# A sparse expert layer in passes of 32 slots on four column tiles, in place of 64 slots on two

## The chip, the cores and the metric

The kernel runs on one core of one Trainium2 chip, as one launch. The metric is the device time of that core in microseconds (us). All data are float32. The profile names the engines PE (TensorE), DVE (VectorE), ACT (ScalarE), POOL (GpSimd) and SP (SyncE, which here only issues DMAs).

## The reference

The model is two blocks over 256 tokens of width 1024. The first block ends in a mixture of 32 experts, of which each token takes 4; the second block is two attention layers, each with an MLP. Only the mixture matters here:

```python
def moe(h, w_router, b_router, w_gate, b_gate, w_up, b_up, w_down, b_down):   # h: 256 x 1024
    logits = h @ w_router + b_router                       # 256 x 32
    top_logit, top_idx = top_k(logits, 4)
    gates = softmax(top_logit)
    # for every expert e, on the tokens xb that chose it:
        g = min(xb @ w_gate[e] + b_gate[e], 7)             # w_gate[e], w_up[e], w_down[e]: 1024 x 1024
        u = clip(xb @ w_up[e] + b_up[e], -7, 7)
        act = g * sigmoid(1.702 * g) * (u + 1)
        y = act @ w_down[e] + b_down[e]
    # y * gate is added to the token's row
```

The 1024 pairs of token and expert are spread unevenly. Counted with the reference's own routing on its inputs, the experts 0 to 31 are chosen by 22, 29, 25, 37, 37, 5, 12, 32, 47, 41, 54, 24, 25, 51, 35, 13, 28, 55, 32, 30, 68, 10, 39, 41, 23, 39, 36, 36, 33, 21, 11 and 33 tokens. One expert (number 20) has more than 64, and 16 have more than 32. The weights of one expert are 3 matrices of 4 MiB.

## The kernel before

**Passes.** An expert's tokens are worked on in passes of `SLOTS` = 64 slots. The number of passes comes from the data: the routing part (lines 1216 to 1255) counts the tokens of every expert, turns the counts into passes per expert and writes a table from which all engines read their loop bounds. With 64 slots there are 33 passes, two for expert 20.

**One pass on TensorE** (`one_pass`, from line 1422): the first product with w_gate (`expand`, L1402), `gather` of the next pass's tokens by a one-hot matrix (L1370), the product with w_up (L1402), the transpose of the gathered tokens (`turn_x`, L1376), the transpose of this pass's gate matrix (L1438), `combine`, which adds the pass before to its tokens (L1412), the transpose of the activations (L1446), the `biases` that open the next pass's sums (L1383), and the product with w_down (L1456).
**The other engines in a pass.** DVE makes the one-hot matrices (L1518, L1522), clips g (L1529) and u (L1531) and multiplies (L1533, L1536). ACT computes the sigmoid (L1496) and copies out of PSUM: xrow (L1498), xs (L1500), selT (L1503), actT (L1505), y (L1507).

**Weights.** They stream through a ring of ten slots (`ring`), each of 2 MiB, called a part: half of one matrix. An expert is six parts, in the order gate 0 and 1, up 0 and 1, down 0 and 1. The parts 1 to 10 in the order of use (all of expert 0, four of expert 1) are loaded while the routing is computed; the other 182 are issued by SP at L1334. SP takes them strictly in order, and before each it waits until the slot is free: until the *last* pass of the expert two back (parts 0 to 3) or one back (parts 4 and 5) has read the part that lies there. An expert with several passes thus keeps its parts until its last pass reads them. After the last part SP issues the loads for the next stage (L1356 to L1361), once the last pass of expert 30 has ended.

**The end.** The last pass is that of expert 31. Behind it come the copy of y and one more `combine` (L1412 at 1128.87), then the second block.

## Time and profile before

| | |
|---|---|
| median of 3 runs | 1847.85 us (1847.38 to 1848.78) |
| the profiled execution | 1845.13 us |
| its span, first to last instruction | 1843.3 us |
| mean granted TensorE clock | 0.996 |
| PE busy | 1799.4 us, 98% of the span |
| expert stage, first product to the end of the last w_down product | 221.4 to 1128.2 us |
| passes in it | 33 |

Everything outside the span is 1.8 us, and the profiled execution was 2.7 us shorter than the median. A busy PE is not PE at its peak, and the share of busy time does not tell by itself which engine or queue sets the time of a stage; that is read from what each waits for.

### The profile page before, as it was taken

The numbers are of one execution on the slowest core, as the hardware profiler recorded it, in microseconds if no ns is written. First come the engines' busy times: TensorE is split into PE (matmuls) and PEld (weight loads), VectorE is DVE, ScalarE is ACT, GpSimd is POOL, SyncE is SP. The second block draws the span as 40 slices with busy tenths as digits, with TensorE's granted clock in tenths as the row PEclk, the third lists the DMA queues.
The fourth block names the chain that finished last, engine by engine and source line by source line (L and its number), as shares of the span: only waits on it lengthen the run. The fifth ranks groups of instructions, "written<-read, shape, count | busy, mean of one in ns | idle before, by whom it ended". The sixth has DMA issues, their size and how long they took to land. (4 is left out here: it accounts for less than half of the span.)

```text
span 1843.3 us, 23681 instructions
## 1 busy us (share of the span) xinstructions
PE 1799.4 (98%) x9487; PEld 1003.5 (54%) x9488; DVE 605.5 (33%) x1262; ACT 371.8 (20%) x721; POOL 10.9 (1%) x14
## 2 busy tenths in 40 slices
PE   7999899999999999999999999999999999999998
PEld 6757533333333333333333335767995466699843
DVE  1854411111111011011011013544655544345555
ACT  3222411111111111111111113332220033222101
POOL 0000000000000000000000000000000000000001
PEclk9999999999999999999999999999999999999999
DMA  9996699999999999999999999432446443124452
GB/s 379 390 191 271 261 418 430 431 431 431 432 432 431 432 431 431 432 431 432 431 431 431 432 431 329 156 142 92 151 149 241 160 182 137 46 92 149 149 176 98
DMA packets 104495, 558.61 MB, mean 303 GB/s; under 512 B 17128, under 2 KB 33997, under 8 KB 78701
## 3 DMA queue, kind: packets, MB, share of 16 engines
q1 hardware_dynamic: 101876, 553.06, 74.3%
q10 hardware_dynamic: 2554, 4.63, 1.8%
q8 instruction: 47, 0.77, 0.2%
q14 instruction: 18, 0.15, 0.0%
HBM read 552.43 MB, written 5.23 MB: 303 GB/s over the span
## 5 line engine op out<-in xcount | busy, mean ns | idle before, releaser
L1402 PE MATMUL ps<-ring,xs 128*64 128x512 f32 x2112 | 465.5, 592 | 4.9 <-DMA ring<-in_w_up 2.5
L1402 PEld LDWEIGHTS ps<-ring,xs 128*64 128x64 f32 x2112 | 151.3, 137 | 307.6 <-issue 298.2
L1456 PE MATMUL ps<-ring,actT 128*64 128x512 f32 x1056 | 233.9, 595 | 0.0
L2274 PE MATMUL ps<-ring 128*128 128x512 f32 x448 | 192.8, 592 | 0.0
L1529 DVE TENSOR_SCALAR hT<-ps 128x512 f32<-128x512 f32 x33 | 22.8, 692 | 446.0 <-PE ps L1402 446.0
L1456 PEld LDWEIGHTS ps<-ring,actT 128*64 128x64 f32 x1056 | 72.9, 137 | 158.7 <-issue 136.8
L2274 PEld LDWEIGHTS ps<-ring 128*128 128x128 f32 x448 | 84.9, 190 | 105.7 <-issue 105.7
L2010 PE MATMUL ps<-hT,ring 128*128 128x256 f32 x512 | 117.9, 383 | 4.3 <-ACT hT L1654 2.9
L1531 DVE TENSOR_SCALAR hT<-ps 128x512 f32<-128x512 f32 x33 | 22.9, 693 | 263.5 <-PE ps L1402 263.5
L2010 PEld LDWEIGHTS ps<-hT,ring 128*128 128x128 f32 x512 | 94.7, 190 | 23.2 <-issue 5.9
L2228 PE MATMUL ps<-hT,ring 128*128 128x128 f32 x768 | 93.4, 275 | 0.2 <-ACT hT L1654 0.2
L2228 PEld LDWEIGHTS ps<-hT,ring 128*128 128x128 f32 x768 | 89.5, 192 | 0.5 <-ACT hT L1654 0.3
L1507 ACT COPY y<-ps 128x512 f32<-128x512 f32 x33 | 19.3, 586 | 246.5 <-PE ps L1456 246.5
L1412 PE MATMUL ps<-selT,y 64*128 64x256 f32 x544 | 67.9, 389 | 0.7 <-ACT y L1507 0.7
L1500 ACT COPY xs<-ps 128x512 f32<-128x512 f32 x33 | 19.4, 587 | 232.4 <-PE ps L1376 232.4
L1370 PE MATMUL ps<-x_sb,sel 128*64 128x512 f32 x272 | 65.7, 605 | 0.4 <-PEq L360 0.4
L2228 PE MATMUL ps<-spare,ring 128*128 128x128 f32 x512 | 62.1, 275 | 0.0
L2228 PE MATMUL ps<-sq,ring 128*128 128x128 f32 x512 | 62.1, 275 | 0.0
L2228 PEld LDWEIGHTS ps<-sq,ring 128*128 128x128 f32 x512 | 59.6, 192 | 0.0
L2228 PEld LDWEIGHTS ps<-spare,ring 128*128 128x128 f32 x512 | 59.6, 192 | 0.0
L1496 ACT ACTIVATE hT<-hT 128x512 f32<-128x512 f32 x33 | 20.8, 630 | 190.0 <-DVE hT L1529 190.0
L2192 PE MATMUL ps<-x_sb,ring 128*128 128x256 f32 x256 | 57.4, 381 | 0.9 <-ACT x_sb L1637 0.9
(455 smaller groups left out, 1812.4 us busy)
## 6 DMA issues: line engine op xcount, KB each, us to landing
ring<-in_w_gate SPq DMA_DIRECT2D x64, 2048.0 KB, 26.2
ring<-in_w_down SPq DMA_DIRECT2D x64, 2048.0 KB, 26.1
ring<-in_w_up SPq DMA_DIRECT2D x64, 2048.0 KB, 24.6
ring<-in_mlp_w SPq DMA_DIRECT2D x16, 2048.0 KB, 8.4
ring<-in_mlp_w SPq DMA_DIRECT2D x32, 1024.0 KB, 5.4
ring<-in_w_mod SPq DMA_DIRECT2D x8, 2048.0 KB, 12.2
ring<-in_odd_w_in SPq DMA_DIRECT2D x6, 2048.0 KB, 10.1
ring<-in_w_mod SPq DMA_DIRECT2D x16, 512.0 KB, 10.9
```

What stands on the lines that cost most here:

```text
L1370: mm = pe.matmul(ps[SLOTS * half:SLOTS * (half + 1), TURN, :], sel[:, i, :], h2[:, i, half * 512:(half + 1) * 512], start=(i == 0), stop=( ...
L1402: mm = pe.matmul(ps[SLOTS * half:SLOTS * (half + 1), bank, :], xs[:, c % 4, c // 4 * SLOTS:(c // 4 + 1) * SLOTS], weights(v, 8 * part + c) ...
L1412: mm = pe.matmul(ps[:, COMB + 2 * half + j // 2, (j % 2) * SEQ:(j % 2 + 1) * SEQ], y[SLOTS * half:SLOTS * (half + 1), j * P:(j + 1) * P], ...
L1456: mm = pe.matmul(ps[SLOTS * half:SLOTS * (half + 1), Y, :], actT[:, f % 4, f // 4 * SLOTS:(f // 4 + 1) * SLOTS], weights(v, 16 + f)[:, hal ...
L1496: act.activation(sig, g, ACT.Sigmoid, scale=ALPHA).then_inc(sig_ok, 1)
L1500: act.copy(xs[:].rearrange("p b n -> p (b n)"), ps[:, TURN, :]).then_inc(xs_sb, 1)
L1529: v.tensor_scalar(g, ps[:, G, :], LIMIT, None, ALU.min).then_inc(g_ok, 1)
L1531: v.tensor_scalar(u, ps[:, U, :], -LIMIT, LIMIT, ALU.max, ALU.min).then_inc(u_ok, 1)
L2010: mm = pe.matmul(ps[:, bank, 0:SEQ], w[:, c, at:at + P], hT[:, c, :], start=(c == 0), stop=(c == C - 1))
L2192: mm = pe.matmul(ps[:, turn.banks[k], (d % 2) * SEQ:(d % 2 + 1) * SEQ], w[c // 4][:, c % 4, d * P:(d + 1) * P], mixT[:, c, :], start=(firs ...
L2228: mm = pe.matmul(out[:, i, :], weight[:, k, i * P:(i + 1) * P], token[:, k, :], start=(opens and k == 0 and i == 0), stop=(k == 3), skip_g ...
L2274: return pe.matmul(product_bank(layer, n), token, weight, start=(c == 0), stop=(c == PAIRS - 1))
```

## The change

`SLOTS` is 32. Every product is split into four quarters of 256 output columns (`WIDE`), each in its own column tile of 32 columns (`QUARTERS` = 4), in every pass of every expert. Experts with more than 32 tokens get a second pass, expert 20 a third. The four matmuls of a group read the same 32 slots' rows and four different quarters of the weights. `combine` works on 32 rows by 128 columns, four row tiles; the transposed activations are produced by plain matmuls with the identity, two column tiles of 64, and are copied by two ACT instructions of 64 partitions; the gate matrix is turned into the free half of bank Y. The zeroing of unused rows ahead of the loop goes. In the routing part the passes per expert are counted by one comparison and one sum in place of a chain of three comparisons.

```diff
-SLOTS = 64
+SLOTS = 32
+QUARTERS, WIDE = P // SLOTS, D // (P // SLOTS)
...
-            v.tensor_scalar(more[:, 1:2], more[:, 0:1], float(SLOTS), 1.0, ALU.is_gt, ALU.add).then_inc(more_chain, 1)
-            for n in range(2, SEQ // SLOTS):
-                v.wait_ge(more_chain, n)
-                v.scalar_tensor_tensor(more[:, 1:2], more[:, 0:1], float(n * SLOTS), more[:, 1:2], ALU.is_gt, ALU.add).then_inc(more_chain, 1)
...
+            v.scalar_tensor_tensor(tmp[:, 2, 0:SEQ // SLOTS], iota[0:EXPERTS, 0:P:SLOTS // 2], 2.0, more[:, 0:1].to_broadcast([EXPERTS, SEQ // SLOTS]),
+                                   ALU.mult, ALU.is_lt).then_inc(more_chain, 1)
+            v.wait_ge(more_chain, 2)
+            v.tensor_reduce(more[:, 1:2], tmp[:, 2, 0:SEQ // SLOTS], AX, ALU.add).then_inc(more_chain, 1)
...
             def gather():
                 for i in range(QT):
-                    for half in range(2):
-                        mm = pe.matmul(ps[SLOTS * half:SLOTS * (half + 1), TURN, :], sel[:, i, :], h2[:, i, half * 512:(half + 1) * 512],
+                    fours = h2[:, i, :].rearrange("p (k n a) -> p k n a", k=2, a=4)
+                    for h in range(QUARTERS):
+                        mm = pe.matmul(ps[SLOTS * h:SLOTS * (h + 1), TURN, 0:WIDE], sel[:, i, :], fours[:, h // 2, :, h % 2 * 2:h % 2 * 2 + 2],
                                        start=(i == 0), stop=(i == QT - 1))
...
+            def turn_act():
+                for a in range(4):
+                    for lane in range(2):
+                        mm = pe.matmul(ps[2 * SLOTS * lane:2 * SLOTS * (lane + 1), TURN, a * P:(a + 1) * P], g[:, a:WIDE:4], ident, start=True, stop=True)
+                mm.then_inc(actT_ps, 1)
...
             def expand(bank, part, v, turn):
                 for c in range(C):
                     if c % 4 == 0:
                         arrived(v, turn, 2 * part + c // 4)
-                    for half in range(2):
-                        mm = pe.matmul(ps[SLOTS * half:SLOTS * (half + 1), bank, :], xs[:, c % 4, c // 4 * SLOTS:(c // 4 + 1) * SLOTS],
-                                       weights(v, 8 * part + c)[:, half * 512:(half + 1) * 512], start=False, stop=(c == C - 1),
+                    at = (c // 4 * 2 + c % 4 // 2) * SLOTS
+                    for h in range(QUARTERS):
+                        mm = pe.matmul(ps[SLOTS * h:SLOTS * (h + 1), bank, 0:WIDE], xs[:, c % 2, at:at + SLOTS],
+                                       weights(v, 8 * part + c)[:, h * WIDE:(h + 1) * WIDE], start=False, stop=(c == C - 1),
                                        skip_group_check=True)
...
                 pe.wait_ge(u_ok, i + 1)
                 pe.wait_ge(selg_ok, i + 1)
-                for j in range(QT):
-                    mm = pe.transpose(ps[:, U, j * P:(j + 1) * P], selg[:, j, :, :].rearrange("p a n -> p (a n)"), ident)
-                mm.then_inc(selt_ps, 1)
+                pe.wait_ge(now_ok, i + 1)
                 pe.wait_ge(y_sb, i + 1)
                 pe.wait_ge(selT_sb, i + 1)
+                for j in range(QT):
+                    mm = pe.transpose(ps[:, Y, WIDE + j * P:WIDE + (j + 1) * P], selg[:, j, :, :].rearrange("p a n -> p (a n)"), ident)
+                mm.then_inc(selt_ps, 1)
                 combine(False, comb_ps)
...
             act.wait_ge(xt_ps, 1)
-            act.copy(xs[:].rearrange("p b n -> p (b n)"), ps[:, TURN, :]).then_inc(xs_sb, 1)
-            for half in range(2):
-                rest = slice(SLOTS * half + EXPERTS, SLOTS * (half + 1))
...
+            act.copy(xs[:].rearrange("p b n -> p (b n)"), ps[:, TURN, 0:WIDE]).then_inc(xs_sb, 1)
+            act.sem_inc(y_sb, 1)
+            act.sem_inc(selT_sb, 1)
...
                 act.wait_ge(actT_ps, i + 1)
-                act.copy(actT[:].rearrange("p b n -> p (b n)"), ps[:, TURN, :]).then_inc(actT_sb, 1)
+                for lane in range(2):
+                    rows = slice(64 * lane, 64 * (lane + 1))
+                    turned = ps[rows, TURN, :].rearrange("p (a q s) -> p a q s", q=2, s=SLOTS)[:, :, lane, :]
+                    act.copy(actT[rows].rearrange("p b (k s) -> p (b k) s", k=2), turned).then_inc(actT_sb, 1)
                 act.wait_ge(down_ps, i + 1)
-                act.copy(y[:], ps[:, Y, :]).then_inc(y_sb, 1)
+                act.copy(y[:], ps[:, Y, 0:WIDE]).then_inc(y_sb, 1)
```

The order of TensorE's instructions from the end of the second product to the first half of the third in a pass of the kernel before, with what each waits for (e_u_ok is DVE's clipped u, e_y_sb and e_selT_sb are ACT's copies of the pass before, part_in4 and part_in5 are the parts with w_down):

```order
L1376 MATMUL ps<-consts_sb,xrow 128x128 [waits e_xrow_sb]
L1376 MATMUL ps<-consts_sb,xrow 128x128 x3
L1438 MATMUL ps<-consts_sb,selg 128x128 [waits e_selg_ok,e_u_ok]
L1438 MATMUL ps<-consts_sb,selg 128x128
L1412 MATMUL ps<-selT,y 128x256 [waits e_selT_sb,e_y_sb]
L1412 MATMUL ps<-selT,y 128x256 x7
L1446 MATMUL ps<-consts_sb,hT 128x128 [waits e_act_ok,e_xs_sb]
L1446 MATMUL ps<-consts_sb,hT 128x128 x3
L1383 MATMUL ps<-brows,now 64x512 [waits e_selT_sb,e_now_ok]
L1383 MATMUL ps<-brows,now 64x512 x3
L1456 MATMUL ps<-ring,actT 64x512 [waits part_in4,e_actT_sb]
L1456 MATMUL ps<-ring,actT 64x512 x7
```

The same stretch of TensorE in the changed kernel (its lines are a few higher, and hT holds the activations):

```order
L1376 MATMUL ps<-consts_sb,xrow 128x128 [waits e_xrow_sb]
L1376 MATMUL ps<-consts_sb,xrow 128x128
L1448 MATMUL ps<-consts_sb,selg 128x128 [waits e_y_sb,e_now_ok,e_selT_sb,e_selg_ok,e_u_ok]
L1448 MATMUL ps<-consts_sb,selg 128x128
L1419 MATMUL ps<-selT,y 128x256 x8
L1382 MATMUL ps<-consts_sb,hT 64x128 [waits e_act_ok,e_xs_sb]
L1382 MATMUL ps<-consts_sb,hT 64x128 x7
L1389 MATMUL ps<-brows,now 32x256 x8
L1455 ISA
L1460 MATMUL ps<-ring,actT 32x256 [waits part_in4,e_actT_sb]
L1460 MATMUL ps<-ring,actT 32x256 x15
```

The steps keep their order. A product has twice as many matmuls of half the columns and half the slots, `turn_x` two transposes in place of four, the activations eight matmuls in place of four transposes; the waits for y and selT stand one step earlier, and the biases no longer wait for selT's copy.

## Rows read from the trace of the kernel before

**Rows 1.** The page's costliest groups: line, engine, shapes, count; busy, mean; idle before.
```profile
L1402 PE MATMUL ps<-ring,xs 128*64 128x512 f32 x2112 | 465.5, 592 | 4.9 <-DMA ring<-in_w_up 2.5
L1456 PE MATMUL ps<-ring,actT 128*64 128x512 f32 x1056 | 233.9, 595 | 0.0
L1507 ACT COPY y<-ps 128x512 f32<-128x512 f32 x33 | 19.3, 586 | 246.5 <-PE ps L1456 246.5
```
**Rows 2.** Stretches: length, busy time of each engine, TensorE clock, DMA share, GB/s.
```profile
230.00:1090.00 860.00, 852.77 (x4318) 324.06 (x4314) 118.64 (x281) 144.45 (x219) 0.00 (x0) 1.00 1.01 431
230.00:400.00 170.00, 169.30 (x858) 64.33 (x856) 22.77 (x54) 28.37 (x43) 0.00 (x0) 1.00 1.00 427
850.00:1090.00 240.00, 238.92 (x1206) 90.30 (x1202) 32.03 (x75) 40.45 (x61) 0.00 (x0) 1.00 1.01 431
```
**Rows 3.** PE in order of time, the last pass: start, length, work, idle before.
```profile
1100.68 7.04 PE L1402 MATMUL ps<-ring,xs 128*64 128x512 f32 x32
1107.55 1.89 PE L1370 MATMUL ps<-x_sb,sel 128*64 128x512 f32 x8
1109.27 7.04 PE L1402 MATMUL ps<-ring,xs 128*64 128x512 f32 x32
1116.23 0.74 PE L1376 MATMUL ps<-consts_sb,xrow 128*128 128x128 f32 x4
1117.10 0.44 PE L1438 MATMUL ps<-consts_sb,selg 128*128 128x128 f32 x2
1117.46 2.00 PE L1412 MATMUL ps<-selT,y 64*128 64x256 f32 x16
1119.39 0.74 PE L1446 MATMUL ps<-consts_sb,hT 128*128 128x128 f32 x4
1120.08 1.09 PE L1383 MATMUL ps<-brows,now 32*64 32x512 f32 x8
1121.10 7.09 PE L1456 MATMUL ps<-ring,actT 128*64 128x512 f32 x32
1128.87 2.00 PE L1412 MATMUL ps<-selT,y 64*128 64x256 f32 x16 [0.69 <-ACT y L1507]
```
**Rows 4.** Issues of SP in order of time, first and last loads of the experts.
```profile
225.12 3.76 SPq L1334 DMA_DIRECT2D ring<-in_w_down  x2
279.79 3.76 SPq L1334 DMA_DIRECT2D ring<-in_w_down  x2
1076.99 3.76 SPq L1334 DMA_DIRECT2D ring<-in_w_down  x2
```
**Rows 5.** Issue to landing of the loads issued at 225.1, 279.8, 1077.0, 1080.4 us.
```profile
ring<-in_w_down SPq DMA_DIRECT2D x1, 2048.0 KB, 7.9
ring<-in_w_down SPq DMA_DIRECT2D x1, 2048.0 KB, 13.8
ring<-in_w_down SPq DMA_DIRECT2D x1, 2048.0 KB, 34.2
ring<-in_w_down SPq DMA_DIRECT2D x1, 2048.0 KB, 35.7
```
**Rows 6.** PE in the first stage: four column tiles of 32, and what follows.
```profile
32.60 3.66 PE L455 MATMUL ps<-ring 128*32 128x256 f32 x64
36.20 1.13 PE L474 MATMUL ps<-hT,ring 128*128 128x256 f32 x4
```
**Rows 7.** Groups by form: weight loads of `combine`, and ACT's copy of 256 columns.
```profile
L1412 PEld LDWEIGHTS ps<-selT,y 64*128 64x128 f32 x528 | 48.3, 186 | 10.0 <-issue 5.6
L1503 ACT COPY selT<-ps 128x256 f32<-128x256 f32 x33 | 12.3, 372 | 64.7 <-PE ps L1412 64.7
```
**Rows 8.** PE ahead of the first pass, in order of time.
```profile
214.36 3.46 PE L1370 MATMUL ps<-x_sb,sel 128*64 128x512 f32 x8 [0.43 <-PEq L360]
221.43 7.09 PE L1402 MATMUL ps<-ring,xs 128*64 128x512 f32 x32 [1.48 <-issue]
```
**Rows 9.** Stretches of the routing part, columns as in rows 2 (clock third from last).
```profile
203.00:206.00 3.00, 1.91 (x13) 1.43 (x11) 2.96 (x15) 1.02 (x4) 0.00 (x0) 1.00 0.12 49
206.00:209.00 3.00, 3.00 (x15) 2.24 (x14) 2.79 (x12) 0.00 (x0) 0.00 (x0) 0.70 0.33 68
215.00:217.00 2.00, 2.00 (x8) 0.54 (x4) 0.00 (x0) 0.00 (x0) 0.00 (x0) 0.50 0.22 66
195.00:198.00 3.00, 2.87 (x22) 1.42 (x20) 2.71 (x5) 2.62 (x6) 0.00 (x0) 1.00 1.02 437
```

More of the change, by code:

```diff
@@ L353, in stage_first @@
     base = scratch((PASSES,), EXPERTS)
-    gate_rows = [m.selT[SLOTS * half:SLOTS * half + EXPERTS, :, :].rearrange("e i n -> e (i n)") for half in range(2)]
+    gate_rows = [m.selT[SLOTS * h:SLOTS * (h + 1), :, :].rearrange("e i n -> e (i n)") for h in range(QUARTERS)]
     pick = m.pick[0:EXPERTS, :]
@@ L1374, in turn_x @@
             def turn_x():
-                for b in range(4):
-                    mm = pe.transpose(ps[:, TURN, b * P:(b + 1) * P], xrow[:, b:512:4], ident)
+                for b in range(2):
+                    mm = pe.transpose(ps[:, TURN, b * P:(b + 1) * P], xrow[:, b:WIDE:2], ident)
                 mm.then_inc(xt_ps, 1)
+            def turn_act():
[3 more added lines that the diff above has]
+                mm.then_inc(actT_ps, 1)
             def biases(parts):
-                for half in range(2):
+                for h in range(QUARTERS):
                     for part, bank in parts:
                         a = EXPERTS * part
-                        mm = pe.matmul(ps[SLOTS * half:SLOTS * (half + 1), bank, :], now[a:a + EXPERTS, :],
-                                       m.brows[a:a + EXPERTS, half * 512:(half + 1) * 512], start=True, stop=False,
+                        mm = pe.matmul(ps[SLOTS * h:SLOTS * (h + 1), bank, 0:WIDE], now[a:a + EXPERTS, :],
+                                       m.brows[a:a + EXPERTS, h * WIDE:(h + 1) * WIDE], start=True, stop=False,
                                        skip_group_check=True)
@@ L1408, in combine @@
             def combine(stop, done):
-                for j in range(4):
-                    for half in range(2):
-                        mm = pe.matmul(ps[:, COMB + 2 * half + j // 2, (j % 2) * SEQ:(j % 2 + 1) * SEQ],
-                                       y[SLOTS * half:SLOTS * (half + 1), j * P:(j + 1) * P],
-                                       selT[SLOTS * half:SLOTS * (half + 1), :, :].rearrange("p i n -> p (i n)"),
+                for j in range(2):
+                    for h in range(QUARTERS):
+                        mm = pe.matmul(ps[:, COMB + h, j * SEQ:(j + 1) * SEQ],
+                                       y[SLOTS * h:SLOTS * (h + 1), j * P:(j + 1) * P],
+                                       selT[SLOTS * h:SLOTS * (h + 1), :, :].rearrange("p i n -> p (i n)"),
                                        start=False, stop=stop, skip_group_check=True)
@@ L1454, in one_pass @@
                         arrived(v, turn, 4 + f // 4)
-                    for half in range(2):
-                        mm = pe.matmul(ps[SLOTS * half:SLOTS * (half + 1), Y, :], actT[:, f % 4, f // 4 * SLOTS:(f // 4 + 1) * SLOTS],
-                                       weights(v, 16 + f)[:, half * 512:(half + 1) * 512], start=(f == 0), stop=(f == C - 1),
+                    for h in range(QUARTERS):
+                        mm = pe.matmul(ps[SLOTS * h:SLOTS * (h + 1), Y, 0:WIDE], actT[:, f % 4, f // 4 * SLOTS:(f // 4 + 1) * SLOTS],
+                                       weights(v, 16 + f)[:, h * WIDE:(h + 1) * WIDE], start=(f == 0), stop=(f == C - 1),
                                        skip_group_check=True)
@@ L1479, in _ @@
         def _(act):
[L1480 to L1481 removed]
+            for h in range(QUARTERS):
+                act.dma_start(y[SLOTS * h:SLOTS * (h + 1), :], t["b_down"][0][:, WIDE * h:WIDE * (h + 1)]).then_inc(bdown_in, 16)
             act.wait_ge(x_ps, 1)
[L1483 removed]
+            act.copy(xrow[:], ps[:, TURN, 0:WIDE]).then_inc(xrow_sb, 1)
             act.wait_ge(xt_ps, 1)
[L1485 to L1492 removed]
+            act.copy(xs[:].rearrange("p b n -> p (b n)"), ps[:, TURN, 0:WIDE]).then_inc(xs_sb, 1)
+            act.sem_inc(y_sb, 1)
+            act.sem_inc(selT_sb, 1)
             n = passes(act)
@@ L1512, in _ @@
             iota = cst(m, "iota", P, 0, SLOTS)
-            twice = iota.rearrange("p (a n) -> p a n", a=1).to_broadcast([P, 2, SLOTS])
+            times = iota.rearrange("p (a n) -> p a n", a=1).to_broadcast([P, QUARTERS, SLOTS])
             with v.Fori(0, n) as i:
```

69 lines of the change are left out of this document (27 added, 42 removed).

## The prediction

> **What bounds the kernel now.** I read the page's costliest groups first. The two products of the experts hold 699 of the 1843 us, and the 4.9 us of idle time ahead of L1402 are the only ones they have [rows 1]. By that alone TensorE is the bound, and halving a pass would give much. Then I read the stretches of the expert stage. PE is busy for 852.8 of 860 us, but the DMA engines stand at a share of 1.01 and 431 GB/s over the same 860 us [rows 2]. Both are full. Which of them is ahead shows only in the landings. The stage needs 182 parts of 2.097 MB after the first ten; the first lands at 225.1 + 7.9 = 233.0, the last at 1080.4 + 35.7 = 1116.1 [rows 4, 5]. TensorE starts the last part half way through the last w_down product, at 1121.1 + 3.5 = 1124.6, and ends at 1128.2 [rows 3]. So the stream ends only 8.5 us before its last part is used. One expert takes the stream 6 x 4.87 = 29.2 us and TensorE 27.3 (1100.68 to 1128.0 in rows 3, 33 times); the ten parts loaded ahead and the second pass of expert 20 are what TensorE lives on. What the change can win in the products is covered by the stream; what counts is when the stream starts, whether it is ever interrupted, and what TensorE still has to do when the last part has landed.
>
> **The rate of the stream.** The 13th load lands at 279.8 + 13.8 = 293.6, the 181st at 1077.0 + 34.2 = 1111.2: 817.6 / 168 = 4.867 us per part. Before the 13th it is slower: 293.6 - 233.0 = 60.6 us for 12, where 12 x 4.867 = 58.4. The stream runs at 427 GB/s there and at 431 later [rows 2], since slots come free one by one at TensorE's pace.
>
> **A pass of the changed kernel.** Four column tiles with 256 columns are in the trace already: 64 records in 3.60 us until the next matmul starts (36.20 - 32.60) [rows 6]. A part is 16 matmuls, 32 records: 1.80 us, where it was 3.45. Six parts are 10.8, and `gather` with 16 records 0.9. The rest stands between the second product and the third: `turn_x` 0.4 (two of four transposes [rows 3]); some 0.15 until DVE has clipped u; the two gate transposes 0.37; `combine`; the activations 0.95 (4 pairs of 128 columns, each like half a record pair of 256 columns, with gaps); and ACT's two copies after them, 2 x 0.37 [rows 7], which the biases (0.7) no longer cover, so 0.75. `combine` has no row of its form. By the streams of four concurrent row tiles it takes 2 x 0.45 + 0.1 = 1.0; by its 16 weight loads, which fill 48.3 / 33 = 1.46 us a pass now [rows 7], 1.7. I take 1.3, between them. Sum of the middle: 3.9. A pass is 15.6 us, with 15.1 and 16.2 as ends.
>
> The Trainium skill ("TensorE: Matmul & The Clock Gate", LDWEIGHTS) says a weight load costs by its columns and not its rows, 128 / 1.2 = 107 ns; 16 of them make 1.7 us, so four row tiles would win nothing over two. The 1.46 us of the present 16 loads agree roughly. With it the pass is 16.0 and the sum below 1.2 us higher (0.4 each at expert 20, in the tail and in the last `combine`).
>
> **How many passes.** By the counts 15 experts have one, 16 two, one three: 49. 49 x 15.6 = 764 us is under the stream's 182 x 4.867 = 886, so TensorE waits for parts over a hundred us in all. The longest run of two-pass experts is four (25 to 28): 4 x 31.2 = 125 us against 117. The lag of 8 us fits in the slots: a two-pass expert frees its first part 3.6 us after its last landed, and as a load issued on an empty queue lands after 7.9 [rows 5], it would have to be late by 24.3 - 3.6 - 7.9 = 12.8 us before the stream stops (24.3 is five landings, four loads being under way).
>
> **The sum,** on the axis of the profiled execution:
> - *Start of the stream.* Ahead of the first pass `gather` falls from 3.46 to about 1.8 [rows 8], two copies lose 0.2 each; I put the first product at 219.5 in place of 221.4. The first slot is free after one part: 1.8 (clock high) or 3.6 (clock low) in place of 3.45, hence 3.6 or 1.8 us earlier. I take 2.9. More copies of the gate rows and wider tables cost tenths beside other waits; nothing.
> - *Early gaps* of the stream, 60.6 - 58.4 = 2.2 us, go, as slots now come free at twice the pace.
> - *Expert 20.* It keeps its six parts for three passes. The other four slots fill in 19.5 us after its last part landed, while its first part comes free 1.8 + 15.6 + 1.8 = 19.2 after, and that load lands at 27.1 where 24.3 was due: the stream loses 2.8.
> - Last landing: 1116.1 - 2.9 - 2.2 + 2.8 = 1113.8.
> - *The tail.* Expert 31 has 33 tokens, so behind the last landing stand the second half of w_down (1.8) and a whole second pass (15.6), for one token; before, 12.1 us stood there. Plus 0.6 for a low clock in it (below): 1131.8 against 1128.2, +3.6.
> - The copy of y has half the columns (0.59 to 0.37 [rows 1, 7]), the last `combine` 1.3 for 2.0: -0.9.
>
> Together +2.7 us: the profiled time would go from 1845.1 to 1847.8, and the median of the runs from 1847.85 to 1850.6. The next stage's loads are queued behind the last part as now, and its first products wait for ACT, not for them.
>
> **The clock.** In the routing part TensorE was busy for 1.91 of 3 us, with small matmuls; the next 3 us show a granted clock of 0.70, and later 2 us at 0.50, which is 1.2 GHz, with `gather` at twice its time [rows 8, 9]. The changed kernel's one-pass experts work 1.8 us in each 4.87, less than that. At 1.2 GHz a part takes 3.6, still under 4.87, so it is hidden there; a second pass may begin low and lose up to 1.8 us, if its first part is read at that clock. In the last one I count a third of it, 0.6.
>
> The Trainium skill ("TensorE: Matmul & The Clock Gate", HAM oscillation) has a kernel whose work per loaded tile is shorter than the wait for the next, and which began every tile at the low clock. By that each first pass runs at 1.2 GHz, 29 to 31 us, as long as an expert's loads; this is the second rival. Rows 9 point that way; no row shows it in a loop like this one.
>
> **Rivals.**
> 1. *TensorE's passes come out longer than some 16.8 us.* No row has more than 64 of these short records in one piece; a pass has 144, and about twice the instructions in little more than half the time. At 17.5 us the run of four lags 23 us, 10 beyond the slots' slack; with 1.9 more at expert 20 and 1.9 more in the tail, less what the 15.6 had: about +16. Against it: 57 ns per record held for all 64 in rows 6. Should it cost as much as today (27.3), 49 passes last 1338, +430.
> 2. *The clock stays low through first passes.* The middle does not halve its waits, and a first pass takes about 30; two-pass experts then need 30 + 16 = 46 less what overlaps the arrivals, and lag from the second on. I count 9 to 18, +12.
> 3. *The other side: the stream gets faster.* It ran at 437 GB/s while PE was busy with small matmuls in the routing part [rows 9]. If a TensorE that pauses leaves room, 881 us x (1 - 431 / 437) = 12 us go: -9. It decides from 433 GB/s on. Against it: 431 in every long stretch, with the engines' share at 1.01.
> 4. *The change does less than it says:* the passes stay long enough that the tail alone counts, with no early start: +3.6 + 2.9 + 2.2, +8.
>
> **How the numbers follow.** Forecast 0.66, of its own -0.5 to +6; rival 1 0.09; rival 2 0.11; rival 3 0.07; rival 4 0.07. A measurement tells a difference of 0.2%, 3.7 us, from none. Of the forecast's cases three in four lie under 3.7: 0.50 same, 0.16 slower. With the rivals: faster 0.08 (rival 3, and a little of the forecast), same 0.50, slower 0.42. The range runs from 1846.0 to 1865.0, with both ends of the pass, and rivals 2 and 4 and the lower part of 1 in it.
>
> **What would show it.** A step from one part to the next of 4.87 us with PE idle on DMA in one-pass experts, over 100 us in all; 49 sigmoids on ACT; a pass without waits of 15.6 us; the DMA share below 1 only for some 3 us around expert 20; the last part landing near 1114 and the last w_down product ending near 1132; a clock below 1 in one-pass experts. Wrong it is if the last landing is later than 1118 (TensorE holds slots), or before 1108 (the stream is faster), or if a pass is over 17.

## The result

The changed kernel takes 1865.49 us in the median (1864.04 to 1866.27, 5 runs), the kernel before 1847.85 (1847.38 to 1848.78): a ratio of 1.0088 with a 95% interval of 1.0076 to 1.0100. It is slower by 17.6 us by the two medians, and by 16.3 by the ratio. The prediction had 1850.6 and "no change" as its likeliest answer, with 0.42 on slower; the measured median lies 0.5 us above the upper end of its range, while the time by the ratio, 1864.1, lies just inside it. The profiled execution took 1866.27 us with a span of 1864.5, 21.2 more than the span of before; why this pair of profiles differs by more than the medians is told under the start of the stream, below.

The costliest groups of the page, and its line on fetched instructions (columns as in [rows 1]; for the queue: packets, MB, share of 16 engines):

```profile
L1409 PE MATMUL ps<-ring,xs 128*32 128x256 f32 x6272 | 393.6, 405 | 110.2 <-issue 45.5
L1460 PE MATMUL ps<-ring,actT 128*32 128x256 f32 x3136 | 181.2, 381 | 20.2 <-ACT actT L1507 13.6
L1495 ACT ACT_TABLE_LOAD x49 | 62.9, 1283 | 1.8 <-issue 1.0
L1509 ACT COPY y<-ps 128x256 f32<-128x256 f32 x49 | 18.2, 372 | 194.2 <-PE ps L1460 194.2
```

```profile
q8 instruction: 118, 1.93, 0.4%
```

Against [rows 1] the two products fell from 699 to 575 us of busy time, though there are 49 passes for 33, and the idle time ahead of the first of them rose from 4.9 to 110.2. Of that, 45.5 us are "issue": TensorE waits there for nothing that the profile shows. The same queue of before is one of the page's lines that I had not read:

```profile
q8 instruction: 47, 0.77, 0.2%
```

The stretch of the expert stage, and those in it in which the DMA engines fall behind (columns as in [rows 2]):

```profile
230.00:1110.00 880.00, 752.81 (x12148) 433.80 (x12140) 130.31 (x422) 183.66 (x374) 0.00 (x0) 0.95 1.00 425
518.00:524.00 6.00, 6.00 (x119) 3.64 (x112) 0.09 (x1) 1.66 (x2) 0.00 (x0) 1.00 0.77 292
812.00:818.00 6.00, 5.62 (x92) 3.38 (x88) 2.35 (x8) 1.48 (x4) 0.00 (x0) 1.00 0.82 350
818.00:824.00 6.00, 6.00 (x116) 3.57 (x112) 0.20 (x1) 1.66 (x2) 0.00 (x0) 1.00 0.45 137
```

425 GB/s stand where 431 stood [rows 2], and the granted clock is 0.95. Two breaks are visible. Stretches of 6 us below 418 GB/s, each counted by what it lacks to 431, add up to 2.3 us in 518 to 530 and 5.8 in 812 to 830, which is expert 20 with its three passes; 8.8 us from 230 to 1130.

TensorE in order of time (start, length, work, idle before): around the first product, at three of five like places, in a one-pass expert, where both products wait for their parts, and the last pass.

```profile
218.79 1.94 PE L1370 MATMUL ps<-x_sb,sel 128*32 128x256 f32 x16 [0.30 <-PEq L361]
224.03 3.66 PE L1409 MATMUL ps<-ring,xs 128*32 128x256 f32 x64 [0.86 <-issue]
...
278.86 1.93 PE L1409 MATMUL ps<-ring,xs 128*32 128x256 f32 x32 [2.95 <-DMA ring<-in_w_gate]
283.66 2.97 PE L1409 MATMUL ps<-ring,xs 128*32 128x256 f32 x32 [1.96 <-DMA ring<-in_w_up]
...
354.67 6.02 PE L1409 MATMUL ps<-ring,xs 128*32 128x256 f32 x64 [7.13 <-issue]
503.06 5.22 PE L1409 MATMUL ps<-ring,xs 128*32 128x256 f32 x64 [6.78 <-issue]
781.37 6.00 PE L1409 MATMUL ps<-ring,xs 128*32 128x256 f32 x64 [7.00 <-issue]
...
1134.23 3.64 PE L1409 MATMUL ps<-ring,xs 128*32 128x256 f32 x64
1137.68 1.09 PE L1370 MATMUL ps<-x_sb,sel 128*32 128x256 f32 x16
1138.59 3.63 PE L1409 MATMUL ps<-ring,xs 128*32 128x256 f32 x64
1142.15 0.50 PE L1376 MATMUL ps<-consts_sb,xrow 128*128 128x128 f32 x2
1142.77 0.44 PE L1448 MATMUL ps<-consts_sb,selg 128*128 128x128 f32 x2
1143.14 1.15 PE L1419 MATMUL ps<-selT,y 32*128 32x256 f32 x16
1144.22 1.23 PE L1382 MATMUL ps<-consts_sb,hT 128*64 128x128 f32 x16
1145.38 0.66 PE L1389 MATMUL ps<-brows,now 32*32 32x256 f32 x16
1146.30 3.66 PE L1460 MATMUL ps<-ring,actT 128*32 128x256 f32 x64 [0.27 <-ACT actT L1507]
1150.46 1.15 PE L1419 MATMUL ps<-selT,y 32*128 32x256 f32 x16 [0.49 <-ACT y L1509]
```

The last rows are [rows 3] in the new form: a pass of 1149.96 - 1134.23 = 15.7 us, where 27.5 stood. The stalls of some 7 us come every five experts, where TensorE's turn loop jumps back, and the product behind each runs at the low clock first (5.2 to 6.1 us over all five, for 3.66). Against [rows 4, 5], SP's first and last issues and their landings are:

```profile
226.02 2.13 SPq L1333 DMA_DIRECT2D ring<-in_w_down  x2
...
1086.96 2.06 SPq L1333 DMA_DIRECT2D ring<-in_w_down  x2
```

```profile
ring<-in_w_down SPq DMA_DIRECT2D x1, 2048.0 KB, 7.8
ring<-in_w_down SPq DMA_DIRECT2D x1, 2048.0 KB, 43.7
```

So the first load lands at 226.0 + 7.8 = 233.8, and the last, the second of its pair, at 1088.7 + 43.7 = 1132.4. It had been 233.0 and 1116.1. From these four numbers and the end of the last w_down product the account of the two profiled executions closes:

| from to | before | forecast | after | forecast of the difference | measured |
|---|---|---|---|---|---|
| first landing | 233.0 | 230.1 | 233.8 | -2.9 | +0.8 |
| first to last landing | 883.1 | 883.7 | 898.6 | +0.6 | +15.5 |
| last landing to end of w_down | 12.1 | 18.0 | 17.6 | +5.9 | +5.5 |
| last copy and `combine` | | | | -0.9 | -1.0 |
| sum | | | | +2.7 | +20.8 |

The span grew by 21.2. Everything except the second row came out within 4 us; the second row missed by 14.9. The question for the chip was what makes a stream of loads 15.5 us longer when TensorE is idle for over a hundred microseconds beside it.

### The profile page after: what moved, and what is told of

Read it like the earlier page. It is cut to its first block and busy times, and to the rows that moved or that the text cites. A ratio compares the mean times of both kernels' runs of the same rounds, so it can differ in the third digit from the quotient of the medians.

```text
span 1864.5 us, 40823 instructions
## 1 busy us (share of the span) xinstructions
PE 1694.5 (91%) x17687; PEld 1119.9 (60%) x17688; DVE 616.4 (33%) x1405; ACT 409.8 (22%) x880; POOL 10.9 (1%) x14
## 3 DMA queue, kind: packets, MB, share of 16 engines
q8 instruction: 118, 1.93, 0.4%
## 5 line engine op out<-in xcount | busy, mean ns | idle before, releaser
L1409 PE MATMUL ps<-ring,xs 128*32 128x256 f32 x6272 | 393.6, 405 | 110.2 <-issue 45.5
L1409 PEld LDWEIGHTS ps<-ring,xs 128*32 128x32 f32 x6272 | 212.4, 116 | 279.2 <-issue 90.1
L1460 PE MATMUL ps<-ring,actT 128*32 128x256 f32 x3136 | 181.2, 381 | 20.2 <-ACT actT L1507 13.6
L1531 DVE TENSOR_SCALAR hT<-ps 128x256 f32<-128x256 f32 x49 | 20.8, 425 | 462.1 <-PE ps L1409 462.1
L1460 PEld LDWEIGHTS ps<-ring,actT 128*32 128x32 f32 x3136 | 96.3, 110 | 105.1 <-ACT actT L1507 31.4
L1533 DVE TENSOR_SCALAR hT<-ps 128x256 f32<-128x256 f32 x49 | 20.8, 425 | 239.4 <-PE ps L1409 239.4
L1495 ACT ACTIVATE hT<-hT 128x256 f32<-128x256 f32 x49 | 20.4, 417 | 218.4 <-DVE hT L1531 218.4
L1499 ACT COPY xs<-ps 128x256 f32<-128x256 f32 x49 | 18.3, 372 | 216.9 <-PE ps L1376 216.9
L1509 ACT COPY y<-ps 128x256 f32<-128x256 f32 x49 | 18.2, 372 | 194.2 <-PE ps L1460 194.2
L1382 PEld LDWEIGHTS ps<-consts_sb,hT 128*64 128x64 f32 x784 | 50.9, 207 | 16.3 <-issue 16.3
L1382 PE MATMUL ps<-consts_sb,hT 128*64 128x128 f32 x784 | 60.2, 296 | 0.0
```

The source lines that it names most:

```text
L1382: mm = pe.matmul(ps[2 * SLOTS * lane:2 * SLOTS * (lane + 1), TURN, a * P:(a + 1) * P], g[:, a:WIDE:4], ident, start=True, stop=True)
L1409: mm = pe.matmul(ps[SLOTS * h:SLOTS * (h + 1), bank, 0:WIDE], xs[:, c % 2, at:at + SLOTS], weights(v, 8 * part + c)[:, h * WIDE:(h + 1) * ...
L1460: mm = pe.matmul(ps[SLOTS * h:SLOTS * (h + 1), Y, 0:WIDE], actT[:, f % 4, f // 4 * SLOTS:(f // 4 + 1) * SLOTS], weights(v, 16 + f)[:, h * ...
L1495: act.activation(sig, g, ACT.Sigmoid, scale=ALPHA).then_inc(sig_ok, 1)
L1531: v.tensor_scalar(g, ps[:, G, 0:WIDE], LIMIT, None, ALU.min).then_inc(g_ok, 1)
L1533: v.tensor_scalar(u, ps[:, U, 0:WIDE], -LIMIT, LIMIT, ALU.max, ALU.min).then_inc(u_ok, 1)
```

## The experiments

Three theories stood for it: TensorE's stalls at the jump hold slots; expert 20 and the runs of two-pass experts hold slots; or something takes time of the DMA engines themselves. Several of the runs leave tokens or products out, to take a piece of work away; the expectations say which. Each ratio below is against the kernel before on the same chip; "stream" is the time from the first to the last landing of the loads after the first ten, in the profiled execution, of which each kernel has one. How far such a number can be trusted shows in kernels that share the turn loop: 898.6 in the changed kernel and 898.2 in `l_last1`, 894.4, 894.0 and 894.5 in `u_straight`, `s_swap` and `s_late`.

### The turn loop written out

```diff
-            with pe.Fori(0, EXPERTS // TURN_EXPERTS) as turn:
-                for v in range(TURN_EXPERTS):
-                    first = first_pass(pe, bass.ds(turn * TURN_EXPERTS + (PASSES + 1 + v), 1), v)
-                    expert(v, turn, first, first_pass(pe, bass.ds(turn * TURN_EXPERTS + (PASSES + 2 + v), 1)))
+            for e in range(EXPERTS - EXPERTS % TURN_EXPERTS):
+                expert(e % TURN_EXPERTS, e // TURN_EXPERTS, first_of(pe, e), first_of(pe, e + 1))
```

> The changed kernel with TensorE's loop over turns of five experts written out as straight code for 30 experts (the loop over an expert's passes stays). Theory (code fetch): the body of five experts no longer stays where TensorE reads its code, is fetched anew in each turn, and the jump back costs the 6.6 to 7.3 us of idle 'issue' time seen five times, plus 2.4 us of low clock behind it. Without the jump no such idle time stands; the stream's break at 518 us (2.3 us) goes and that at expert 20 falls from 5.8 to about 2.7; 5 us less than the changed kernel (4 to 7), 1860.5. Instruction bytes stay near 1.9 MB. Rival (slots): the breaks come from experts with two and three passes holding their slots, whatever the loop: within 1 us of 1865.5. Rival (fetching competes with the stream): time falls only if instruction bytes fall.

Measured: 1860.57 us (1858.95 to 1862.11), ratio 1.0073 (1.0056 to 1.0090), 4.9 below the changed kernel's median (by the two ratios, from separate series, 2.8, with intervals that overlap). The five stalls are gone (issue time ahead of the first product falls from 45.5 to about 10.5), and so is the break at 518. The stream is 894.4, 4.2 shorter. The break at expert 20 stays:

```profile
806.00:812.00 6.00, 5.63 (x92) 3.40 (x84) 2.35 (x8) 1.48 (x4) 0.00 (x0) 1.00 0.68 292
812.00:818.00 6.00, 6.00 (x120) 3.60 (x113) 0.00 (x0) 1.66 (x2) 0.00 (x0) 1.00 0.41 150
```

These two and the next stretch lack 6.7 us, where the expectation had some 2.7, so expert 20's break is not made by a jump. The jumps hold slots, but by either number cost less than a third of the 17.6 us.

### The kernel before with turns of ten experts

```diff
-            with pe.Fori(0, EXPERTS // TURN_EXPERTS) as turn:
-                for v in range(TURN_EXPERTS):
+            with pe.Fori(0, 3) as turn:
+                for v in range(10):
```

The expert's slot group stays `v % TURN_EXPERTS`; the turn number is `turn * 2 + v // TURN_EXPERTS`.

> The kernel before with turns of ten experts in place of five, three turns in place of six: the same work with a loop body twice as long, about as many bytes as five experts of the changed kernel. Code fetch: instruction bytes rise from 0.77 to about 1.7 MB, and at the two jumps back a 7 us fetch less the 4 us that TensorE's queue holds stands as idle 'issue' time, 3 to 4 us each; as TensorE has little slack in this kernel, 3 to 8 us slower, 1851 to 1856. Rival (the short passes or the 32-column form make the stalls): no new idle time, within 1 us of 1847.9.

Measured: 1855.48 us (1852.40 to 1859.29), ratio 1.0040 (1.0027 to 1.0054). At both jumps TensorE now stalls in the old form of the kernel too, with the low clock behind it (8.79 for the 7.04 of [rows 3]):

```profile
505.08 8.79 PE L1402 MATMUL ps<-ring,xs 128*64 128x512 f32 x32 [3.76 <-issue]
...
785.10 8.79 PE L1402 MATMUL ps<-ring,xs 128*64 128x512 f32 x32 [4.05 <-issue]
```

The stall comes with the larger body of the loop, and not with tiles of 32. Fetched instructions went from 0.77 to 1.29 MB, less than the 1.7 expected, and the stream from 883.1 to 889.5 with only two stalls in it. That was the first sign that the fetching itself costs.

### Expert 20 capped at two passes

```diff
-            v.tensor_scalar(more[:, 0:1], ps[0:EXPERTS, 5, 0:1], 1.0, None, ALU.max)
+            v.tensor_scalar(more[:, 0:1], ps[0:EXPERTS, 5, 0:1], 1.0, 64.0, ALU.max, ALU.min)
```

> The changed kernel with the count of tokens capped at 64 when passes are counted, so that expert 20 has two passes in place of three; its last 4 pairs are left out. Slots theory: the break of the weight stream around 812 to 830 us, 5.8 us, goes; time 5.8 less, 1859.7. Rival (code fetch alone makes the break): the 7 us stall ahead of expert 20 stays, its first part comes free well before the queue runs dry, so the two agree on the break; they differ if the break does not go: then 1865.

Measured: 1861.97 us (1859.93 to 1863.43), ratio 1.0074 (1.0057 to 1.0091), stream 895.3. Expert 20's break is gone, but smaller ones stand later, in the run of four two-pass experts:

```profile
818.00:824.00 6.00, 5.52 (x100) 3.17 (x104) 0.06 (x1) 1.66 (x2) 0.00 (x0) 1.00 1.01 434
1022.00:1028.00 6.00, 6.00 (x116) 3.31 (x104) 0.42 (x1) 0.85 (x3) 0.00 (x0) 1.00 0.90 339
1052.00:1058.00 6.00, 6.00 (x116) 3.53 (x112) 0.42 (x1) 2.45 (x4) 0.00 (x0) 1.00 0.92 360
```

The third pass is worth 3.3 us of the stream, close to the forecast's 2.8; the expectation of 5.8 failed. The visible break at expert 20 (5.8 us) was larger than what went with it.

### Expert 31 with one pass

```diff
-            v.tensor_scalar(more[:, 0:1], ps[0:EXPERTS, 5, 0:1], 1.0, None, ALU.max)
+            v.tensor_copy(more[:, 0:1], ps[0:EXPERTS, 5, 0:1])
...
+            v.scalar_tensor_tensor(more[:, 2:3], more[:, 3:4], 30.5, more[:, 0:1], ALU.is_lt, ALU.mult).then_inc(one_chain, 1)
...
+            v.tensor_scalar(more[:, 0:1], more[:, 2:3], 1.0, None, ALU.max).then_inc(one_chain, 1)
```

`more[:, 3:4]` holds the expert's index; the count of expert 31 becomes 1.

> The changed kernel with one pass for expert 31 in place of two; its one pair above 32 is left out, and two small DVE instructions are added in the routing part (+0.3 us). Tail theory: the whole second pass, 15.7 us from product to product, stands behind the last landing; 15.4 less than the changed kernel, 1850. Rival (the next stage waits for its own loads, which queue behind the last part and land later): TensorE would wait ahead of the first product of the second block, and the gain would be 3 to 8 us.

Measured: 1856.56 us (1853.27 to 1857.71), ratio 1.0050 (1.0034 to 1.0067), 8.9 below the changed kernel's median, and 7.0 by the ratios. The end of the last w_down product comes 2.2 us behind the last landing instead of 17.6, so 15.4 us of the tail are gone, and about half of that comes back. What is late next is in two views. TensorE in order of time:

```profile
1132.22 1.15 PE L1424 MATMUL ps<-selT,y 32*128 32x256 f32 x16 [0.49 <-ACT y L1514]
1137.74 2.07 PE L2039 MATMUL ps<-acc,consts_sb 128*128 128x256 f32 x4 [4.38 <-ACT acc L2450]
```

and SP's issues (start, time that the issue held SP):

```profile
1101.23 25.25 SPq L1361 DMA_DIRECT2D ring<-in_even_w_in  x1
...
1133.46 3.21 SPq L1365 DMA_DIRECT2D ring<-in_even_w_in  x1
1137.06 4.65 SPq L1900 DMA_DIRECT2D ring<-in_even_w_in  x1
```

The last `combine` is over at 1133.4, but TensorE's first work of the next stage starts at 1137.7. SP, which issues the next stage's loads at the end of the experts' block, comes out of that block only at 1136.7, 7.1 us after the last part landed. With the second pass in place this wait was hidden behind it. The first twelve matmul records there also take 5.3 us instead of 3.0 (their lengths added up), as TensorE stood idle before them and starts at the low clock. Against the 0.99 us of idle time that the changed kernel has at this place, the wait is worth 3.4 us and the clock 2.3: 15.4 - 5.7 = 9.7 us are the net price of the second pass, as an estimate from the two profiles.

### Experts 30 and 31 exchanged

Expert 30 has one pass. Here the whole computation is done, with the turn loop written out and the two last experts exchanged:

```diff
+ROW_MOVES = ((0, 0, 30), (30, 31, 1), (31, 30, 1))
...
+    e = {30: 31, 31: 30}.get(e, e) if isinstance(e, int) else e
```

The counts, the gate columns and the bias rows are exchanged in the same way; b_down is loaded by SP.

> u_straight with the experts 30 and 31 worked on in the other order (logits, bias rows and weight loads exchanged; b_down is loaded by SP), so that the last expert is the one with 21 tokens and one pass. The computation is complete. Tail theory: behind the last landing stand 2.2 us of TensorE in place of 17.5; but in l_last1 the next block began only 7.1 us after the last landing, when SP had issued the last load of the next stage, and at a low clock. So 12 us of 15 come back, less 2: 10 less than u_straight, 1850.6. Rival (SP's issuing is no bound): 15 less, 1845. Rival (the tail is hidden anyway): 1860.

Measured: 1849.23 us (1847.54 to 1852.24), ratio 1.0012 (1.0002 to 1.0021). Its tail is 3.6 us, its stream 894.0. TensorE's wait ahead of the next stage is 1.40 us here, against 4.38 in `l_last1`, and its clock is high behind it, so most of the 13.9 us that the tail is shorter than in `u_straight` comes back as time: 11.3. (Expert 30 has 11 tokens; the 21 of the expectation are expert 29's.) This is the best complete kernel with 32 slots, 14 us below the changed one by the ratios, and it still does not beat the kernel before.

### The next stage's loads issued behind the block

The kernel of the exchange, with four loads of the next stage moved from SP's end of the experts' block to its start of the next block:

```diff
-            sp.dma_start(columns(16), src[:, :, NQ:NQ + 512]).then_inc(m.even_in[1], 16)
...
+            for k, (a, lo) in enumerate(((16, NQ), (20, MQ), (0, MK))):
+                sp.dma_start(columns(a), src[:, :, lo:lo + 512]).then_inc(m.even_in[k + 1], 16)
```

> s_swap with four of the five next-stage loads (L1356 to L1360) issued by SP at the start of the second block in place of the end of the expert stage. If the end of the expert stage waits for SP, whose issues block until queued loads drain, the first product of the second block comes some 3 to 5 us earlier than in s_swap, 1846.5; if those loads' landing is what counts, they now land later and it is up to 8 us slower than s_swap.

Measured: 1857.49 us (1857.09 to 1857.97), ratio 1.0058 (1.0041 to 1.0074), 8.3 worse than the kernel that it is made from: the rival was right. SP is out of its block sooner, which saves 0.4 us of TensorE's wait ahead of the next stage (0.99 for 1.40), but the loads land later, and that counts. TensorE waits for them in the next stage and goes on at the low clock, where the kernel with the exchange alone had no wait and 3.94 us:

```profile
1161.83 5.49 PE L2028 MATMUL ps<-ring,hT 128*128 128x280 f32 x16 [4.24 <-DMA ring<-in_even_w_in]
```

```profile
1123.00:1129.00 6.00, 5.89 (x100) 3.37 (x92) 1.31 (x4) 1.16 (x3) 0.00 (x0) 1.00 1.01 419
1129.00:1135.00 6.00, 5.73 (x104) 3.66 (x108) 0.39 (x1) 1.11 (x3) 0.00 (x0) 1.00 0.64 245
```

After 1129 the DMA engines stand at a share of 0.64, with work that could have been queued. These terms make 4.24 + 1.55 - 0.4 = 5.4 us. The two profiles differ by 8.6; the other 3.1 stand before the end of the last w_down product, as `gather` began at 218.9 and not at 215.5, a difference that the edit does not reach (see the start, below). So 5 us of the 8.3 are shown to come from the loads.

### All experts with one pass, and a quarter of the products

Now TensorE is taken out of the stream's way altogether.

```diff
-            v.tensor_scalar(more[:, 0:1], ps[0:EXPERTS, 5, 0:1], 1.0, None, ALU.max)
+            v.tensor_scalar(more[:, 0:1], ps[0:EXPERTS, 5, 0:1], 1.0, 32.0, ALU.max, ALU.min)
```

> The changed kernel with counts capped at 32: one pass for every expert, all pairs above 32 of an expert left out. Slots theory: no break of the stream above 1 us anywhere, though the five 7 us stalls stand. First to last landing: 881.5 us as in the kernel before without its early gaps, plus 2.6 if the 1.2 MB of fetched code only take their share of the DMA engines (884), or 886 to 888 if the fetches sit on few engines and hold up each part's landing. The end comes 2.2 us after the last landing, the next block 7.1 after it; some 26 us less than the changed kernel, 1839.

Measured: 1852.01 us (1850.14 to 1854.13), ratio 1.0027 (1.0016 to 1.0038). The expectation of 1839 failed by 13 us, that of 884 to 888 for the stream by 6 or more, and this was the run that changed the theory. TensorE waits for parts for 250 us, so it is hardly able to hold the stream up, and yet the stream takes 893.6 us. At its end the engines of the DMA are half idle while the last part, which lands at 1127.1, is still awaited:

```profile
1118.00:1124.00 6.00, 6.00 (x54) 2.89 (x46) 1.28 (x3) 0.37 (x1) 0.00 (x0) 0.54 0.51 218
```

The same with fewer of TensorE's instructions, `range(1)` for the four column quarters in the three products:

```diff
-                    for h in range(QUARTERS):
+                    for h in range(1):
```

> p_cap32 with only the first of the four column quarters of the three products computed, so that the code of five experts is 84 KB or less and stays resident, as in the kernel before. Instruction bytes fall to 0.7 MB, no stalls at the jumps. If fetched code is what slows the stream, first to last landing 881 to 882, 3 to 6 less than p_cap32; if it is not, the same as p_cap32 within 1.

Measured: 1837.97 us (1837.79 to 1838.99), ratio 0.9951 (0.9933 to 0.9968), with no stall at a jump and a stream of 881.4 us. Both kernels load the same weights, and the DVE and ACT work is alike. The stream was expected 3 to 6 us shorter; it is 12.2. Between them lie also the three quarters of TensorE's products and the queue of instructions:

```profile
q8 instruction: 46, 0.75, 0.2%
```

against, in the kernel with all quarters,

```profile
q8 instruction: 114, 1.87, 0.4%
```

The stage of `p_cap32` and of `p_quarter`, in this order:

```profile
230.00:1110.00 880.00, 587.46 (x8016) 296.87 (x8010) 85.80 (x278) 120.74 (x246) 0.00 (x0) 0.86 1.01 429
230.00:1110.00 880.00, 592.11 (x3627) 269.68 (x3627) 87.52 (x282) 122.06 (x250) 0.00 (x0) 0.87 1.01 431
```

429 GB/s for 431 over 880 us are only some 4 of the 12.2 us. Most of the rest is lost just before the last part lands: 358 GB/s from 1112 to 1118, then the 218 above.

### A dose of code, with and without TensorE's work

Half of the quarters (`range(2)`):

> p_cap32 with two of the four column quarters of the three products computed: 84 matmuls a pass in place of 132, about 107 KB of code for five experts, between the 88 KB of the kernel before (resident) and 169 KB (fetched anew). Theory (code size decides): either instruction bytes are 0.75 MB, no idle time at the jumps and 881 to 882 us from first to last landing as in p_quarter, or they are above 1.3 MB with idle time at the jumps and 887 to 891. Rival (what TensorE reads and computes slows the stream): about 885, half way between p_quarter and p_cap32, whatever the instruction bytes.

Measured: 1846.20 us (1844.63 to 1848.70), ratio 0.9984 (0.9974 to 0.9995), 1.54 MB fetched, stalls of 6.2 to 6.4 us at the jumps, stream 889.1, as the theory had it (887 to 891) and not the rival (885). One quarter with the turn loop written out: the same work as `p_quarter`, but more code and no jumps.

> p_quarter with the 30 experts written out as straight code: the same work and the same waits, only 0.4 MB more code is fetched (25 bodies of 15 KB), without any jump back. If fetched code lengthens the stream by 12 us for 1.12 MB, here by 4 to 5: 886 us from first to last landing, and time 1842 to 1843. Rival (the longer stream of p_cap32 came from TensorE's work or from the jumps): 881.4 and 1838 as in p_quarter.

Measured: 1840.84 us (1840.42 to 1843.10), ratio 0.9960 (0.9947 to 0.9973), 1.15 MB, stream 885.5 where 886 was expected (the time is 1.2 us under the expected 1842 to 1843). And the kernel before, written out:

> The kernel before with the 30 experts written out as straight code: 0.45 MB more code is fetched and no jump back is left. If fetching alone lengthens the stream (12 us for 1.12 MB, so 5 here), TensorE waits for parts longer around 722 to 790 us and towards the end, where it had 8.5 us to spare: 2 to 4 us slower than before, 1850 to 1852. Rival (only jumps cost): 1848, as before.

Measured: 1850.15 us (1848.09 to 1852.22), ratio 1.0013 (1.0003 to 1.0023), 1.25 MB, stream 887.2; the time is the one expected.

| kernel | fetched, MB | stream, us | what it shows |
|---|---|---|---|
| `p_quarter` | 0.75 | 881.4 | TensorE never in the way |
| before | 0.77 | 883.1 | |
| `q_straight` | 1.15 | 885.5 | +4.1 for 0.40 MB, same work as `p_quarter` |
| `b_straight` | 1.25 | 887.2 | +4.1 for 0.48 MB, same work as before |
| `b_ten` | 1.29 | 889.5 | two stalls, TensorE with little room |
| `p_half` | 1.54 | 889.1 | |
| `u_straight` | 1.74 | 894.4 | the changed kernel's work, no stall at a jump |
| `p_cap32` | 1.87 | 893.6 | +12.2 for 1.12 MB over `p_quarter` |
| `c_cap64` | 1.95 | 895.3 | with two-pass experts |
| changed | 1.93 | 898.6 | with the third pass of expert 20 |

The two pairs that differ in nothing but the written-out loop have no stall at a jump and the same products, so neither TensorE's work nor its stalls explain their 4.1 us. A megabyte of fetched code costs the stream 9 to 11 us. At 431 GB/s its bytes alone would take 2.3. By the profile's own time for its packets it is some 3.7, as an estimate: 1.18 MB in `p_cap32` take 0.5% of the 16 engines' time over the 880 us of the stage. The times of whole runs go the same way, less sharply: by the ratios `q_straight`, `p_half` and `p_cap32` are 1.7, 6.1 and 14.0 us above `p_quarter`, the first of them not clear of the noise.

The 0.51 above suggests why the cost is that high: if blocks of code fall on some of the 16 engines while each part of 2 MB is spread over all, a part has landed only when the slowest of them is done, and the others run ahead until the queue ends. Which engines fetch the code no view showed, so this last step is argued and not shown.

## Why the prediction was wrong, step by step

By its own sign the prediction is wrong: the last landing was to come no later than 1118, and it came at 1132.4. That the time lies at the very edge of the range is luck, as the upper part of the range was there for rivals 1 and 2, and neither happened.

**A pass, the clock in first passes, the number of passes: right.** Forecast 15.6 us a pass, measured 15.7; 49 sigmoids on ACT; 1.15 us for `combine` where 1.3 was taken, so the 1.7 that the prediction worked out beside it from the columns of the weight loads does not hold here. (Its split into "15 experts have one, 16 two, one three" makes 50; by the counts 16 have one, 15 two and one three, which is the 49 of the sum.) Each record kept its 57 ns through whole passes, which ends rival 1. The steps from part to part in one-pass experts are waits for DMA of 2 to 3 us (278.86 and 283.66 above), and the parts there take 1.93 to 3.6 us by the clock. Rival 2 is out too: it had two-pass experts lag by 9 to 18 us, and they are worth 1.7 of the stream (`p_cap32` to `c_cap64`); `p_cap32`, with its clock at 0.54 in places, still waits for parts 250 us.

The Trainium skill ("TensorE: Matmul & The Clock Gate", HAM oscillation) says that a loop whose work per tile is shorter than its wait for the next one starts its tiles at the low clock. The trace agrees in part: 2.97 us for a part at 283.66, but 1.93 at 278.86, one part earlier. In the stage a cost of it shows only in products behind a jump.

**The tail: right.** 18.0 us forecast behind the last landing, 17.6 measured. `l_last1` adds what the forecast did not see: without the pass there is a wait for SP and a low clock behind it, so taking 15.4 us of tail away gives some 7 to 10. In `s_swap`, where SP was through sooner, the wait is short and most of the tail comes back.

**The start: off by 3.7 us, in part by chance of the profile.** `gather` did fall, from 3.46 to 1.94 us [rows 8]. But it began at 218.79 and not at 214.36, since the clock in the routing part fell sooner. The stretch that had 1.00 in [rows 9] now has

```profile
203.00:206.00 3.00, 3.00 (x10) 2.55 (x10) 2.35 (x18) 2.25 (x6) 0.00 (x0) 0.50 0.63 268
```

The low clock there is not made by the change: `b_ten` has the routing part of the kernel before as it is, and shows it too. The start of `gather` moves between kernels without pattern: 214.4 before, 214.8 in `l_last1`, 215.9 in `u_straight`, 218.8 in the changed kernel, `b_ten` and `c_cap64`, 218.9 in `p_half`. Executions of one and the same kernel differ in the same way: of 22 runs of the kernel before on one chip, ten show a mean clock of 0.993 or 0.994 and take 1849.3 to 1852.1 us, twelve show 0.996 or 0.997 and take 1844.9 to 1849.5. Two single profiles cannot keep up to 4.6 us of this apart from the change. It also fits that the profiles differ by 21.1 us and the medians by 17.6.

**The stream: wrong by 14.9 us, the step that failed.** The forecast took 883.1 - 2.2 + 2.8. Its two small terms were about right. From one kernel to the next:

- before to `p_quarter`: -1.7, the early gaps (forecast -2.2);
- `p_quarter` to `p_cap32`: +12.2, the fetched code, with three quarters of TensorE's products added beside it (forecast: nothing, no term); at 9 to 11 us a megabyte the 1.12 MB make 10 to 12, as an estimate;
- `p_cap32` to `c_cap64`: +1.7, two-pass experts with their lag (forecast 0);
- `c_cap64` to the changed kernel: +3.3, the third pass of expert 20 (forecast 2.8).

Together +15.5. The terms are not independent, and the small ones stand on one profile each. Writing the loop out takes 4.2 off the stream, though by its 0.19 MB less code alone it would be about 2, and the other half may be what the jumps did to the slots, which no run separates.

So the step that failed is the line "Last landing: 1116.1 - 2.9 - 2.2 + 2.8": it let the stream run at its old rate wherever slots were free, and had no term for what the instructions take of it. The sign that the prediction gave for a late landing, TensorE holding slots, is not the main cause either. The mistake was to treat the instruction stream as free. The prediction counted how many instructions TensorE gets, about twice as many, and asked only how fast TensorE works through them. It never asked where they come from, though the page has the line. From this line and the sizes an estimate was possible. A pass of the kernel before has 276 PE instructions by the records of the trace, a pass of the changed kernel 520. With the loop written out the stage (230 to 1110) fetches 0.59 MB in `b_straight` and 1.06 in `u_straight`: 0.47 MB for 30 times 244 further instructions, 64 bytes each. A body of five experts is then 88 KB against 166 KB; `p_quarter` has 74 KB by the same count, `p_half` 105 (the expectations have 84, 107 and 169, by slightly larger counts). Bodies of 74 and 88 KB show no stall at the jump, one of 105 KB does. The limit lies between 88 and 105 KB, as an estimate from instruction counts. Beyond it every turn is fetched again, and each jump back stalls: in the stage the kernel before fetches 0.11 MB, the changed kernel 1.25.

The Trainium skill ("Runtime: NRT & Kernel Launch", Instruction fetch mechanics) has the mechanism: instructions come in blocks of 16 KiB over a DMA queue, and a taken branch whose target is outside the fetched window stalls until its block has come. This is the rule against the change that the prediction should have weighed. The trace agrees with the block size (1.93 MB in 118 packets are 16 KiB a packet) and with the stall, at 6.6 to 7.3 us. The same section calls the crossing from block to block mostly hidden; here it is hidden on TensorE, but not in a weight stream that has no room, at 9 to 11 us a megabyte. It gives TensorE's buffer as 128 KiB; the body of some 105 KB already stalls.

**Rival 3, a faster stream: out.** 434 GB/s stand in one stretch of 6 us above, but where TensorE pauses most and little code is fetched, in `p_quarter`, the stage runs at 431 GB/s, as before. From first to last landing it has 181 parts in 881.4 us, 4.87 us each, the rate of the kernel before.

**Still open.** The break at expert 20 lacks 5.8 us (6.7 with the loop written out) by the bandwidth, where the slots' arithmetic gives 2.8, and removing it gives back 3.3 of the stream. Perhaps engines that carry no code run dry first and later wait for the others anyway; no run tests that. Open too is which engines fetch the code, and so why a megabyte costs more than its packets' time.

## What to carry to other kernels

When a kernel is bound by its loads, look at the instruction queue as a user of the same engines: smaller tiles double the instructions, and if the loop's body outgrows what stays on the engine, all of it is fetched on every turn (76 packets in the stage for 7). Count the body before cutting tiles, and write a loop out only if it was too large anyway (some 3 to 5 us gained in the changed kernel, some 2 lost in the kernel before). And a partly filled pass costs most behind the last landing: exchanging the last two experts, with the loop written out, was worth some 14 us, the change of tiles nothing.

## What the runs showed of the chip

- TensorE's jump back stalls for 6.6 to 7.3 us in the changed kernel, with a body of some 166 KB (up to 8.4 in `c_cap64`, with the same body), 6.2 to 6.4 with 105 KB in `p_half`, 3.8 and 4.1 in the old form with ten experts a turn, and not at all in `p_quarter` and the kernel before, with 74 and 88 KB. The sizes are estimates. The product behind it starts at the low clock.
- Fetched code slows a saturated stream of 2 MB loads by 9 to 11 us per MB (the table), about four times what its bytes alone would take at 431 GB/s.
- Four row tiles of 32 with 128 output columns and 256 streamed ones (`combine`): 16 weight loads and matmuls in 1.15 us, where 16 with two row tiles of 64 took 2.00 [rows 3]. The 16 loads of the last pass keep the load queue busy for 0.74 us at 184 ns a load on average, where 1.46 a pass stood before, at 186: loads into different row tiles overlap.
- A TensorE that had waited 4.38 us (`l_last1`) began with four matmul records in 2.07 us, which take 1.13 after 0.99 us of waiting (the changed kernel).
- Issuing one load held SP for 25.25 us in `l_last1`, while earlier loads took 43.2 us from issue to landing; there TensorE's next stage started 1.1 us after SP was through.
